# Decode's gate columns fetched in the prompt stage, and the state-space tables built from four powers at a time

## The reference

```python
dt = jnp.exp(log_dt)[:, None]
mag = jnp.exp(lr * dt)
ar, ai = mag * jnp.cos(li * dt), mag * jnp.sin(li * dt)
# fr, fi from ar, ai;  bbr = fr * br - fi * bi;  bbi = fr * bi + fi * br
bu_r = jnp.einsum('ntgi,gpi->ntgp', uf, bbr)
# ... an associative scan over time gives hr, hi
y = jnp.einsum('ntgp,gip->ntgi', hr, c_re) - jnp.einsum('ntgp,gip->ntgi', hi, c_im)
```

## Time and profile before

| what | value |
|---|---|
| time, median of 3 runs | 2453.78 us (2451.07 to 2454.67) |
| the profiled execution's own time | 2447.4 us |
| its span on the core | 2445.6 us |
| busy: PE, DVE, ACT, POOL | 2157.7, 895.2, 715.2, 514.3 us |
| state-space stage | from 80.7 us to about 323 us |
| prompt stage | from 768.4 us to about 1098 us |
| decode stage | from 1099.7 us to about 1274 us |

### The profile page before, as it was taken

The page is one execution under the profiler, slowest core; times in us unless marked ns, Lnnn a source line. Parts: engine busy times, 40 slices in busy tenths (PEclk is TensorE's granted clock), DMA queues, the critical chain, the costliest instruction groups (busy, mean ns, idle before and its releaser), DMA issues. The chain is left out here.

```text
span 2445.6 us, 32920 instructions
## 1 busy us (share of the span) xinstructions
PE 2157.7 (88%) x13512; PEld 1812.2 (74%) x13512; DVE 895.2 (37%) x1752; ACT 715.2 (29%) x1485; POOL 514.3 (21%) x506
## 2 busy tenths in 40 slices
PE   7694969978998898884659999999999999999998
PEld 4453645546554566652449999999999999999997
DVE  2597001105442665642453111345412422422424
ACT  3320300003222576652233222333312311311313
POOL 0250000011112654421112211211121122211120
PEclk8886679989998899996879999999999999999999
DMA  8102042325431321106643111311111111111112
GB/s 319 16 1 75 37 114 38 113 73 185 172 138 39 91 74 52 50 26 228 254 182 97 44 51 45 115 35 44 44 48 48 44 44 44 45 51 44 44 54 78
DMA packets 212870, 201.48 MB, mean 82 GB/s; under 512 B 37327, under 2 KB 194999, under 8 KB 204065
## 3 DMA queue, kind: packets, MB, share of 16 engines
q1 hardware_dynamic: 200926, 131.40, 18.3%
q0 software_dynamic: 9216, 67.11, 7.3%
q10 hardware_dynamic: 2578, 0.88, 0.1%
HBM read 177.62 MB, written 21.58 MB: 81 GB/s over the span
## 5 line engine op out<-in xcount | busy, mean ns | idle before, releaser
L2116 PE MATMUL ps<-tail,tail 128*128 128x356 f32 (+2 forms) x2304 | 756.7, 328 | 9.5 <-POOL tail L2514 9.5
L2118 PE MATMUL ps<-tail,tail 128*128 128x356 f32 (+2 forms) x2304 | 750.7, 326 | 0.0
L2117 PE MATMUL ps<-tail,tail 128*128 128x356 f32 (+2 forms) x2304 | 748.9, 325 | 0.0
L2116 PEld LDWEIGHTS ps<-tail,tail 128*128 128x128 f32 x2304 | 435.5, 189 | 12.1 <-POOL tail L2514 9.7
L2117 PEld LDWEIGHTS ps<-tail,tail 128*128 128x128 f32 x2304 | 435.7, 189 | 2.5
L2118 PEld LDWEIGHTS ps<-tail,tail 128*128 128x128 f32 x2304 | 435.8, 189 | 0.0
L2514 POOL TENSOR_TENSOR tail<-tail,tail 128x1024 fp32r<-128x1024 f32 x96 | 232.4, 2421 | 936.9 <-ACT tail L2361 936.9
L2545 DVE SCALAR_TENSOR_TENSOR tail<-ps,mod,tail 128x346 f32<-128x346 f32 (+2 forms) x120 | 68.7, 573 | 344.3 <-PE ps L2118 334.9
L2361 ACT ACTIVATE tail<-tail 128x1024 fp32r<-128x1024 f32 x96 | 101.0, 1053 | 320.2 <-PE ps L2118 314.3
L1609 POOL TENSOR_SCALAR pr<-pr,row_reciprocals,gT 128x640 f32<-128x640 f32 (+7 forms) x128 | 98.7, 781 | 151.4 <-DVE row_reciprocals L1728 150.5
L1256 PE MATMUL ps<-xT,w1T 128*128 128x512 f32 (+1 forms) x288 | 121.7, 579 | 0.0
(11 more groups left out here) (441 smaller groups left out, 2711.6 us busy)
## 6 DMA issues: line engine op xcount, KB each, us to landing
tail<-in_w_ff SPq DMA_DIRECT2D x64, 512.0 KB, 3.8
wada_late<-in_w_ada SPq DMA_DIRECT2D x32, 512.0 KB, 4.2
wada<-in_w_ada SPq DMA_DIRECT2D x4, 2048.0 KB, 11.9
tail<-in_w_in SPq DMA_DIRECT2D x16, 512.0 KB, 3.7
x_keep<-xT SPq DMA_DIRECT2D x1, 4224.0 KB, 11.5
h_keep<-hT SPq DMA_DIRECT2D x1, 4224.0 KB, 13.4
tail<-x_keep SPq DMA_DIRECT2D x1, 4224.0 KB
xrow<-in_x_prompt SPq DMA_DIRECT2D x8, 512.0 KB, 7.2
```

Source lines behind the costliest of these rows:

```text
L2116: pe.matmul(out, whi[:, kw, :], xlo(kx), start=(i == 0), stop=False)
L2117: pe.matmul(out, wlo[:, kw, :], xhi(kx), start=False, stop=False)
L2118: mm = pe.matmul(out, whi[:, kw, :], xhi(kx), start=False, stop=(i == n - 1))
```

## The change

There are three edits. In the state-space stage `turn_parameters` runs after the first input product and no longer after the second, and ACT's two steps of the parameter chain follow `keep_u(0)` and `keep_u(1)`. The tables G and F are written for four powers in one instruction (128x1024 in place of 128x256); F's ninth power keeps its own six. In decode the gate columns become a tile `gate_columns` that lives from the projections to decode's end; SP stores the gates at step j = 8 of the prompt stage and loads three columns at each of the steps j = 12 to 19, behind that step's weight slice. SP waits for the last of them at the end of the prompt stage, and DVE's wait in decode is gone.

```diff
@@ stage_ssm, PE
-                if i == 1:
+                if i == 0:
                     turn_parameters()
@@ stage_ssm, ACT
                 keep_u(i)
-                if i == 1:
+                if i == 0:
                     act.wait_ge(S["dt_spread"], 1)
...
-                if i == 2:
+                if i == 1:
                     act.wait_ge(S["magnitudes_ready"], 1)
@@ stage_ssm, DVE
-            for k in range(LC):
-                q = LC + 1 + k
-                link(tt(Gre[:, :, k, :], BBre[:, :, :], tG(pr, q, SI), ALU.mult))
-                link(tt(tg, BBim[:, :, :], tG(pi, q, SI), ALU.mult))
-                link(tt(Gre[:, :, k, :], Gre[:, :, k, :], tg, ALU.subtract))
...
+            for k in range(0, LC, 4):
+                ks, q = slice(k, k + 4), LC + 1 + k
+                gr, gi, tg = Gre[:, :, ks, :], Gim[:, :, ks, :], half_of(4)
+                br4, bi4, pr4, pi4 = over_k(BBre[:, :, :], 4), over_k(BBim[:, :, :], 4), powers(pr, q, 4), powers(pi, q, 4)
+                link(tt(gr, br4, pr4, ALU.mult))
+                link(tt(tg, bi4, pi4, ALU.mult))
+                link(tt(gr, gr, tg, ALU.subtract))
...
             dve.sem_inc(S["g_ready"], 1)
-            for l in range(LC + 1):
...
+            for l, m in ((0, 4), (4, 4), (8, 1)):
...
             dve.sem_inc(S["tables_ready"], 1)
@@ stage_prompt, SP
                 sp.dma_start(wada[:, j % 2], e.w_ada[0].rearrange("(k p) n -> p k n", p=P)[:, :, a:a + P]).then_inc(ada_loaded[j % 2], 16)
+                if j == 2 * R:
+                    sp.dma_start(gscr, e.gates[:, T:NT]).then_inc(gates_stored, 16)
+                if 3 * R <= j < 3 * R + NSEQ:
+                    load_wait(sp, gates_stored, 1)
+                    n = j - 3 * R
+                    for br in range(3):
+                        sp.dma_start(e.gd[32 * (n % 4):32 * (n % 4) + 32, n // 4, br:br + 1],
+                                     bass.AP(tensor=gscr.tensor, offset=br * HQ * NS + n * TS, ap=[[NS, HQ], [1, TS]]),
+                                     allow_slow_non_contiguous=True).then_inc(gates_landed, 16)
+            load_wait(sp, gates_landed, 3 * NSEQ)
@@ stage_decode, SP
-            sp.dma_start(gscr, e.gates[:, T:NT]).then_inc(gates_stored, 16)
-            load_wait(sp, gates_stored, 1)
-            for n in range(NSEQ):
-                for br in range(3):
-                    sp.dma_start(gd[32 * (n % M):32 * (n % M) + 32, n // M, br:br + 1], ...
@@ stage_decode, DVE
-                if b == 0:
-                    load_wait(dve, gates_landed, 3 * NSEQ)
```

More of the change, by code:

```diff
@@ L818, in _ @@
             link(dve.tensor_copy(x0[:, :, :, :], bank[2][:, 0:2 * P].rearrange("p (c n j) -> p c n j", c=2, n=NSEQ)))
-            tG = lambda a, k, s: a[:, :, k].unsqueeze(2).to_broadcast([P, NJ, s])
-            tg = t0[:, :, :].rearrange("p j n -> p (j n)")[:, 0:NJ * SI].rearrange("p (j i) -> p j i", i=SI)
-            for k in range(LC):
-                q = LC + 1 + k
-                link(tt(Gre[:, :, k, :], BBre[:, :, :], tG(pr, q, SI), ALU.mult))
-                link(tt(tg, BBim[:, :, :], tG(pi, q, SI), ALU.mult))
-                link(tt(Gre[:, :, k, :], Gre[:, :, k, :], tg, ALU.subtract))
-                link(tt(Gim[:, :, k, :], BBim[:, :, :], tG(pr, q, SI), ALU.mult))
-                link(tt(tg, BBre[:, :, :], tG(pi, q, SI), ALU.mult))
-                link(tt(Gim[:, :, k, :], Gim[:, :, k, :], tg, ALU.add))
@@ L830, in _ @@
-            dve.sem_inc(S["g_ready"], 1)
-            for l in range(LC + 1):
[L832 to L839, removed]
+            over_k = lambda a, n: a.unsqueeze(2).to_broadcast([P, NJ, n, SI])
@@ new lines, in _ @@
+            powers = lambda a, q, n: a[:, :, q:q + n].unsqueeze(3).to_broadcast([P, NJ, n, SI])
+            half_of = lambda n: t0[:, :, :].rearrange("p j n -> p (j n)")[:, 0:NJ * n * SI].rearrange("p (j k i) -> p j k i", k=n, i=SI)
+            for k in range(0, LC, 4):
[5 more added lines that the diff above has]
+                link(tt(gr, gr, tg, ALU.subtract))
+                link(tt(gi, bi4, pr4, ALU.mult))
+                link(tt(tg, br4, pi4, ALU.mult))
+                link(tt(gi, gi, tg, ALU.add))
@@ new lines, in _ @@
+            dve.sem_inc(S["g_ready"], 1)
+            for l, m in ((0, 4), (4, 4), (8, 1)):
+                fre, fim, tg = Fre[:, :, l:l + m, :], Fim[:, :, l:l + m, :], half_of(m)
+                cr4, ci4, pr4, pi4 = over_k(CT[:, 0, :, :], m), over_k(CT[:, 1, :, :], m), powers(pr, l, m), powers(pi, l, m)
+                link(tt(fre, cr4, pr4, ALU.mult))
+                link(tt(tg, ci4, pi4, ALU.mult))
+                link(tt(fre, fre, tg, ALU.subtract))
+                link(tt(fim, cr4, pi4, ALU.mult))
+                link(tt(tg, ci4, pr4, ALU.mult))
+                link(dve.scalar_tensor_tensor(out=fim, in0=fim, scalar=-1.0, in1=tg, op0=ALU.mult, op1=ALU.subtract))
@@ L1443, in stage_prompt @@
         ada_loaded = [sem(f"ada_loaded{i}") for i in range(2)]
+        gates_stored, gates_landed = sem("gates_stored"), sem("gates_landed")
+        gscr = nc.dram_tensor("gate_rows", (3 * HQ, NS), F32, kind="Internal").ap()
         block = c.enter_context(nc.Block())
@@ L1771, in stage_decode @@
         vwin = window_slots(e.vwin, e.kT[:, 0, 512:1024])
-        gd = sb("gd", [P, NBAT, 3])
+        gd = e.gd
         sc = sb("sc", [P, NBK + 1])
@@ L1776, in stage_decode @@
         st = sb("st", [P, 8])
-        gscr = nc.dram_tensor("gate_rows", (3 * HQ, NS), F32, kind="Internal").ap()
         ring_landed = [sem(f"ring_landed{i}") for i in range(NR)]
@@ L1780, in stage_decode @@
         window_values_landed = [sem(f"window_values_landed{i}") for i in range(M)]
-        gates_stored, gates_landed, first_scores_done, first_scores_kept, blocks_summed, selection_step, keys_turned, keys_kept_act, keys_kept_dve, scores_done, scores_kept, maxima_done, exps_done, weights_scaled, weights_turned, turned_kept_act, turned_kept_dve, values_read, window_values_read, values_done, outputs_kept = (
-            sem(n) for n in ("gates_stored", "gates_landed", "first_scores_done", "first_scores_kept", "blocks_summed", "selection_step", "keys_turned", "keys_kept_act", "keys_kept_dve", "scores_done",
+        first_scores_done, first_scores_kept, blocks_summed, selection_step, keys_turned, keys_kept_act, keys_kept_dve, scores_done, scores_kept, maxima_done, exps_done, weights_scaled, weights_turned, turned_kept_act, turned_kept_dve, values_read, window_values_read, values_done, outputs_kept = (
+            sem(n) for n in ("first_scores_done", "first_scores_kept", "blocks_summed", "selection_step", "keys_turned", "keys_kept_act", "keys_kept_dve", "scores_done",
                              "scores_kept", "maxima_done", "exps_done", "weights_scaled", "weights_turned", "turned_kept_act", "turned_kept_dve", "values_read", "window_values_read", "values_done", "outputs_kept"))
@@ L1800, in _ @@
                 window(n, kwin, window_keys_landed, e.cache_k_win)
-            sp.dma_start(gscr, e.gates[:, T:NT]).then_inc(gates_stored, 16)
-            load_wait(sp, gates_stored, 1)
-            for n in range(NSEQ):
-                for br in range(3):
-                    sp.dma_start(gd[32 * (n % M):32 * (n % M) + 32, n // M, br:br + 1],
-                                 bass.AP(tensor=gscr.tensor, offset=br * HQ * NS + n * TS, ap=[[NS, HQ], [1, TS]]),
-                                 allow_slow_non_contiguous=True).then_inc(gates_landed, 16)
             for n in range(M):
@@ L2730, in stages @@
         e.qbd = sb("qbd", [P, NSEQ, 32])
+        e.gd = sb("gate_columns", [P, 2, 3])
         e.rowidx = sb("rowidx", [P, NSEQ * 2], U32)
```

## The result

| kernel | median of the runs | lowest to highest | runs |
|---|---|---|---|
| before | 2452.57 us | 2451.07 to 2454.67 | 4 |
| changed | 2425.49 us | 2419.17 to 2432.67 | 4 |

The ratio is 0.989, 95% interval 0.9859 to 0.9921: 27.1 us less, where 17.5 were forecast. The profiled execution is the slowest of the four: 2432.67 us, span 2430.8.

A forecast was written before the change was run, and what follows sets the result against it. PE, busy 2157.7 of 2445.6 us, was taken as the bound, with barriers passing on any microsecond saved in an earlier stage. 3.4 + 14.1 = 17.5 us off 2453.8 gave 2436.3, range 2431 to 2443.

The forecast's parts named there:

- Part 1: State-space stage: parameters turned one product earlier, so the sine and powers come 7.1 us earlier; 3.4 us saved with the wide tables.
- part 2: State-space stage: wide tables end at 144.2 to 161.6, before PE's inputs at 180.9; 3.4 us saved, reachable by either edit.
- the first rival: State-space stage: POOL's rotation table becomes the last, at 184.8, and DVE starts 1.7 us later; time 2441.4, chance 8%.
- Behind this point the stage is one chain: State-space stage behind the tables: a single chain, so the 3.4 us saved ahead of it moves everything behind.
- the two terms: State-space tables 3.4 us and decode's gate columns 14.1 us, together 17.5 us saved.
- Part 3: Decode: gate columns loaded earlier remove DVE's 14.11 us wait and PE's 12.80 us stop; 14.1 us saved.
- the fourth rival: Prompt stage: SP becomes the bound, its added issues and landing times come back; 9.9 us slower, 2463.7, chance 3%.
- the second: Decode: the window values hold the last keys up, so 8.6 us are saved in all; time 2445.2, chance 8%.
- third: Decode: another wait of DVE or PE replaces the gate wait; 3.4 us are left, 2450.4, chance 4%.
- the fifth: Decode: PE's clock, no longer dropped, stays up in the rest, about 5 us more; time 2431, chance 5%.
- a spread of the runs like the one shown: Whole kernel: one of the allowances in the forecast's own range, 2432 to 2440.
- The base 2453.8: Whole kernel: median of the runs shown before the change, 2453.78 us, from which the 17.5 us saving was taken.

## Why the prediction was wrong

- **Part 1 and part 2, 3.4 us:** right in mechanism and size. L865, the L862 of the earlier trace rows, waits for PE, 3.3 us earlier, and either edit alone does it. POOL's table ends 1.5 us ahead of its forecast, so the first rival is out: the alternation read from the rows held. The rule of the Trainium skill ("SBUF — State Buffer", "Who interferes with whom") says that a VectorE instruction with two SBUF inputs and a GpSimd instruction that reads SBUF shut each other out for a whole instruction. The rows agree: 1.18 us for a 16-element POOL instruction beside DVE's 1.23, 0.22 with DVE idle.
- **"Behind this point the stage is one chain":** the step that failed. The dependencies are one chain, but the sum took its length as fixed. The output products took 36.7 us at granted clock 0.50 in the profile before. I read the clock of decode and did not look at this stretch. In the changed kernel it took 32.7 and 28.2 us. From the first output product to the projections the mean of the four profiles with the wide tables and nothing added is 85.0 us, that of the three with neither state-space edit 92.1 (77.5 in the one with the earlier turn alone): about 7 us the sum lacks, in single executions. With the clock held up by work on PE, the difference of the two kernels is 16.5 and 16.6 us, near the 17.5 of the sum. So the two terms were right within about 1 us together, and what the sum lacked is the clock in this stretch. Why the edits let it come up more often is not shown.
- **Part 3, 14.1 us:** decode itself gained 16.0 us (mean of six profiles with the gate columns moved, 168.14, against 184.16 of eight without), but the way from the projections to behind the first twenty products of the prompt stage grew by 2.7 (454.3 against 451.6) and the rest of the prompt stage by 0.5; net 12.8. The two waits shown above make up the 2.7: L979's is 14.6 to 15.3 us in the eight profiles and 15.6 to 16.5 in the six, those for `byg` 17.2 to 18.8 and 18.9 to 19.8, in the means 1.3 each. No gate transfer has run by then. The new tile, whose moved addresses the prediction took at 0, is placed that early, but that it is the cause was not tried. The prompt stage did not grow by SP's work, so the fourth rival is out; the second and third are out by the rows of decode. For the fifth, a clock that stays up in decode, the profiles speak: its mean granted clock is 0.765 to 0.790 in the six and 0.738 to 0.764 in the eight. How much of the 2 us above the forecast that is worth was not tried.
- **The base and the range:** "a spread of the runs like the one shown" took 3.6 us from three runs, though the profiled execution, 2447.4 us, already lay 3.7 below the lowest of them. The spread is 25 us, and the range was set too narrow on that. The base 2453.8 is also 5.6 us above the mean of the 29 runs. Of the 8.6 us between the forecast 2436.3 and the mean of the changed kernel's second measurement, 2427.7, these 5.6 are the larger part; the other 3.0 are saving beyond the 17.5. A measurement with 29 runs of the kernel before and 6 of the changed one still leaves 0.9888 to 0.9947, so it can't tell those 3.0 us from nothing; that the clock adds to the saving rests on the profiles and on the state-space edits timed alone (0.9940 to 0.9984, 4 to 15 us, where 3.4 were forecast).

The Trainium skill ("TensorE: Matmul & The Clock Gate", "Part 1: The HAM clock gate") says that the gate goes by how busy PE has been lately, in a rhythm that doesn't begin with the kernel, so that the moment of the rise varies. The runs agree that it varies, and by far more than the page has it, so the measurement decides here: on the same instructions PE was busy without a gap for all of 36.7 us at 1.2 GHz in four profiles and for about 7 us in another.

## What to carry to other kernels

Look up the granted clock of every stretch in which PE is the chain, and ask of any edit ahead of it whether it moves the start; one at 0.50 can shrink to little over half (36.7 to 20.5 us). Where PE idles ahead of such a stretch, unused products that fit into the idle time held its clock up here, and with it the measurement: 24 us of spread became 7, and a difference of 25 us in the medians (20.5 in the means) turned into the 16.5 that the edits are worth. Count them by a measured duration: 32 instead of 22 cost 7 us in either kernel. Where the runs of a kernel fall into two groups, give the mean and the share of each group beside the median, and do not take the spread from three runs.

## What the runs showed of the hardware that was not expected

A PE without a gap in its records can stay at the lower clock for long. In this stretch, groups of products with 128 and with 64 partitions, it stayed at 0.50 for 7 to 36.7 us, and in the same program the moment differs by execution: 28 and 17 us after the first output product in the two profiles of the changed kernel. Started at 1.00, the same products keep it: 1.00 over all of their 20.5 us, in the four profiles with unused products ahead of them.
